# Decay rows of a chunked scan: 128-fold repetition by DMA from a DRAM scratch in place of selector matmuls on TensorE

## The chip, the cores and the metric

The kernel runs on one core of one Trainium2 chip. The metric is the device time of one execution in microseconds. It is given as the median of several runs; a profile is of one further execution. TensorE is called PE (its weight loads PEld), VectorE DVE, ScalarE ACT, GpSimd POOL, SyncE SP.

## The reference

A sequence of 512 tokens of width 1024 goes through two blocks of two layers each. The first block's layer projects the tokens, runs three mixers beside each other (retention, a Mamba-2 scan, attention with forget gates), and projects back. The second block (feed-forward layers and another mixer) is not touched. What matters here is the scan: 16 heads in 2 groups, head width 64, state width 128, chunks of 128 tokens, so 4 chunks.

```python
def step(S, inp):
    xc, ac, bc, cc = inp
    acum = jnp.cumsum(ac, axis=-1)
    seg = acum[..., :, None] - acum[..., None, :]
    Lm = jnp.exp(jnp.where(causal, seg, -jnp.inf))
    cb = jnp.einsum('bign,bjgn->bgij', cc, bc)
    y = jnp.einsum('bgij,bghij,bjghp->bighp', cb, Lm, xc)
    ...
```

For every chunk and head, `seg` is a 128 by 128 matrix of differences of cumulative sums. With one token index on the partitions, the kernel needs `acum` of the other index as a row that stands in all 128 partitions.

## The kernel before

`scan_and_attend` runs once for each of the two layers. Each engine has its own program, and semaphores tie them. PE's matmuls of the input projection (`proj.run`, jobs numbered j, 24 matmuls of 128x256 each for the jobs meant here) are laid between the steps of the scan. Each job writes one of two PSUM banks, and ACT must copy a bank out (`evacuate`) before the second job after it.

The weights come as a stream of units, four jobs to a unit, in two slots. When a unit's last job is done, ACT rounds the next-but-one unit (`round`, line 127, a cast of 128x2048), then POOL subtracts the rounded from the raw weights (`lower`, line 136), and then SP issues the load of the unit after (line 116).

The scan has 8 steps s, one for each chunk c and group g, in the order (0,0), (0,1), (1,0) and so on. In the loop, PE's order in each step is: job A (jv+2+2s), the matmuls of `spread_decay(s + 1)`, job B (jv+3+2s), `outputs(s)`.

- `spread_decay(s)` (line 1169): 8 matmuls, one for each head of the group (the profile shows 16 instructions). The stationary operand is a 16x128 slice of `sel`, a constant with ones in one row; the moving operand is `afm`, the 16 rows of cumulative sums in that chunk. The result, in PSUM banks 4 and 5, is one row of `afm` in all 128 partitions. It waits until ACT has read the banks for the step before.
- `decays(s)` on ACT: 8 activations Relu (line 1347) that read those banks and subtract from the token's own sum, then one Exp over 128x1024 (line 1352), in place in `seg`, which has two buffers. ACT's order in each step is: evacuate A, `decays(s + 1)`, evacuate B, and in every second step (s even) the cast of line 127. From step 3 on ACT loads its function table anew for Exp and for Silu (line 1285).
- `weigh(s)` on DVE (line 1475): multiplies `seg` by the masked products `cb`.
- `outputs(s)` on PE: 8 products of `seg` with x (line 1184), from chunk 1 on the product with the state (1189), and up to chunk 2 the state's new part (1199).
- `combine(s)` on DVE: x times the skip factor (1490), the state's part scaled (1493, reads PSUM) and added (1494), the products added (1495, reads PSUM), the state scaled (1504) and added (1505, reads PSUM). Where a chunk begins, `scale_x` (1467) and `state_input` (1482) follow, and then `weigh(s + 1)`.

`sel` (16x2048, 128 KB) is loaded by SP at the start of the block. `afm` is copied out of PSUM by ACT long before the loop (line 1320). Behind the loop stand the rest of the projection, the norm over the scan's output and the attention.

Of the kernel before, what the change touches and what calls it, by code (L numbers as in the profile page):

```python
# [21 lines left out]
F32 = mybir.dt.float32  # L22
F32R = mybir.dt.float32r
I32 = mybir.dt.int32
ACT = mybir.ActivationFunctionType
AX = mybir.AxisListType

P = 128
T = 512
NT = T // P  # L30
D = 1024
# [11 lines left out]
SH, SP, SG, SN = 16, 64, 2, 128  # L43
HG = SH // SG
# [31 lines left out]
def split3(ap, a):  # L76
    return ap.rearrange("p (a b) -> p a b", a=a)
# [63 lines left out]
def build(nc, dr, out):  # L141
    ctx = ExitStack()
    with ctx:
# [48 lines left out]
        PS = ctx.enter_context(nc.psum_tensor("PS", [P, 8, 512], F32))  # L192
# [23 lines left out]
            return par[:, P2[name][0]:P2[name][1]]  # L216

        phase = [ExitStack()]

        class Arena:  # L220

# [759 lines left out]
        def scan_and_attend(block, l, streams, norm, after):  # L981
# [10 lines left out]
            s_nc, s_ns, s_nu = sem("c_row_loaded"), sem("c_row_activated"), sem("next_ada_used")  # L992
            parts = MixedParts()
            nb = lambda n: sem("ssd_" + n)
            s_sel, s_sv, s_ab, s_ex, s_w1, s_ln = (nb(x) for x in (
                "selectors_loaded", "vector_step", "gate_magnitudes", "gate_exp", "gate_one_plus", "gate_log"))
            s_a, s_lf, s_sm, s_smt, s_ea = (nb(x) for x in (
                "steps_ready", "log_forget_ready", "cumulative_sums", "cumulative_sums_taken", "decays_ready"))
            s_al, s_cv, s_si, s_bt, s_btc = (nb(x) for x in (
                "a_exp", "convolved", "conv_activated", "b_turned", "b_turned_copied"))  # L1000
            s_cb, s_cbm, s_xt, s_xtc, s_xd = (nb(x) for x in (
                "cb_products", "cb_masked", "x_turned", "x_turned_copied", "x_scaled"))
            s_bc, s_sg, s_le, s_we, s_y, s_yt = (nb(x) for x in (
                "log_decay_spread", "log_decay_ready", "decay_ready", "weights_ready", "y_products", "y_taken"))
            s_sd, s_ss2, s_xdd, s_q2, s_r2, s_yn = (nb(x) for x in (
                "state_products", "state_ready", "x_state_scaled", "y_squared", "y_rms", "y_normed"))
            s_tr, s_ev, s_nf = (nb(x) for x in ("y_turned", "y_turned_copied", "negated_copied"))
# [10 lines left out]
            late = A_[:, 0:3 * D + 2 * T + SH * P]  # L1018
# [3 lines left out]
            xdt = split3(late[:, 0:2 * D], 2)  # L1022
            St = split3(late[:, 2 * D:2 * D + 2 * T], 2)
            yt = split3(late[:, 3 * D:3 * D + 2 * T], 2)
            sel = late[:, 4 * D:4 * D + SH * P]
            bcf = split3(m_all[:, 8 * T:12 * T], 4)
            xdd = bcf[:, 0:2, :].rearrange("p a t -> p (a t)")
            fox_v_ = ar.take(4 * T)
# [9 lines left out]
            afm = M[0:SH, 7, :]  # L1038
# [7 lines left out]
            jd, jb, jx, jv, jg, jz, jq, jk, je = (J[x] for x in ("dtf", "bc", "xs", "fv", "fg", "z", "fq", "fk", "out"))  # L1046
            steps = [(c, g) for c in range(NT) for g in range(SG)]
# [13 lines left out]

            @block.sync
            def _(sp):
                sp.dma_start(sel[0:SH, :], dr["sel"]).then_inc(s_sel, 16)
                n = len(stream.units)
                stream.send(sp, RAW, streams.end_in + 2 * SLOTS)
                sp.wait_ge(s_ev, 8)
                if nxt:
                    sp.dma_start(par[:, 0:P1N], of_layer("par1", l + 1)).then_inc(s_par, 16)
                    sp.wait_ge(s_fe, NT)  # L1070
                    sp.dma_start(c_row, dr["c_row"]).then_inc(s_nc, 16)
                    sp.wait_ge(parts.low, 16)
                    for u in range(NEARLY):
                        if u >= 3:
                            sp.wait_ge(s_nu, 2 * (u - 2))
                        sp.dma_start(next_ada[:, u % 3, :], ada_rows(l + 1, u)).then_inc(s_nl[u % 3], 16)
                        stream.send(sp, RAW, streams.end_in + 2 * SLOTS + u + 1)
                else:
                    sp.dma_start(par[:, 0:KD], dr["final_g"]).then_inc(s_par, 16)
                    sp.dma_start(spec[:, 0:C2N], dr["c2"]).then_inc(s_par, 16)  # L1080
                    stream.send(sp, RAW, n)
                for b in range(2):
                    sp.wait_ge(stream.low, n - 1 + b)
                    after.load_first(sp, b)
                sp.wait_ge(s_par, 16 if nxt else 32)
# [21 lines left out]
            def _(pe):  # L1107
# [3 lines left out]
                for c in range(NT):  # L1111
                    last = pe.transpose(PS[:, 7, c * 24:(c + 1) * 24], dtfT[:, c * P:(c + 1) * P],
                                        ident[0:24, 0:24])
# [8 lines left out]
                for c in range(NT):  # L1122
                    last = pe.matmul(PS[0:SH, 5, c * P:(c + 1) * P], aa[:, c, :], triu, start=True, stop=True)
# [32 lines left out]
                    if j - jx >= 2:  # L1156
                        turn_x(j - jx - 2)

                def spread_decay(s):
                    c, g = steps[s]  # L1160
                    if s == 0:
                        pe.wait_ge(s_sel, 16)
                        pe.wait_ge(s_xtc, 8)
                        pe.wait_ge(s_smt, 3)
                    else:
                        pe.wait_ge(s_sg, s)
                    for h in range(HG):
                        hh = g * HG + h
                        last = pe.matmul(PS[:, 4 + h // 4, (h % 4) * P:(h % 4 + 1) * P],
                                         sel[0:SH, hh * P:(hh + 1) * P], afm[:, c * P:(c + 1) * P],  # L1170
                                         start=True, stop=True)
                    last.then_inc(s_bc, 1)

                def outputs(s):
                    c, g = steps[s]
                    pe.wait_ge(s_we, s + 1)
# [22 lines left out]
                        pe.matmul(PS[:, 2 + g, :], bt[:, g, c, :], xdd[:, g * T:(g + 1) * T],  # L1199
                                  start=True, stop=True).then_inc(s_sd, 1)  # L1200

                spread_decay(0)
                for s in range(8):
                    proj.run(pe, jv + 2 + 2 * s, tokens)
                    if s + 1 < 8:
                        spread_decay(s + 1)
                    proj.run(pe, jv + 3 + 2 * s, tokens)
                    outputs(s)
                for j in range(jz + 2, jq + 2):
# [56 lines left out]
            def _(act):  # L1266
# [61 lines left out]
                for g in range(SG):  # L1328
                    act.wait_ge(s_bt, g + 1)
                    act.copy(bt[:, g, :, :], split3(PS[:, 4 + g, 0:384], 3)).then_inc(s_btc, 1)  # L1330
                for j in range(jx, jv + 2):
                    evacuate(j)
                    if 1 <= j - jx < 9:
                        activate(4 + j - jx - 1)
                    if j - jx >= 3:
                        copy_x(j - jx - 3)
                copy_x(7)

                def decays(s):


                    c, g = steps[s]
                    act.wait_ge(s_bc, s + 1)
                    if s >= 2:
                        act.wait_ge(s_y, s - 1)
                    for h in range(HG):
                        last = act.activation(seg[:, s % 2, h * P:(h + 1) * P],
                                              PS[:, 4 + h // 4, (h % 4) * P:(h % 4 + 1) * P], ACT.Relu,
                                              bias=acum[:, c, g * HG + h:g * HG + h + 1], scale=-1.0)
                    last.then_inc(s_sg, 1)  # L1350
                    act.wait_ge(s_sg, s + 1)
                    act.activation(seg[:, s % 2, :], seg[:, s % 2, :], ACT.Exp, scale=-1.0).then_inc(s_le, 1)

                act.wait_ge(s_rn2, 1)
# [1550 lines left out]
def constants():  # L2905

    f = np.float32
    i = np.arange(P)
    c0 = np.zeros((P, C0N), f)
    c0[:, 0:128] = np.eye(P)  # L2910
    c0[:, 128:256] = 1.0
    c0[:, 256:384] = i[:, None] <= i[None, :]
    c0[:, 768:896] = np.where(i[None, :] > i[:, None], -BIG, 0.0)
    c0[:, 896] = (10000.0 ** (-(i % 64) / 64.0)).astype(f)
    c0[:, 897] = np.where(i < 64, -1.0, 1.0)
    c0[:, 899] = 1.0 / (2 * P)
    c0[:, 900] = 1.0 / D
    c1 = np.zeros((P, C1N), f)
    lg = np.log(1.0 - 2.0 ** (-5.0 - np.arange(RH)))
    diff = i[None, :] - i[:, None]  # L2920
    for h in range(RH):
        c1[:, h * P:(h + 1) * P] = np.where(diff >= 0, np.exp(lg[h] * np.maximum(diff, 0)), 0.0) * P ** -0.5
        c1[:, 512 + h * P:512 + (h + 1) * P] = np.exp(lg[h] * (i + 1.0))[None, :]
        c1[:, 1024 + h] = np.exp(lg[h] * (P - 1.0 - i)) * P ** -0.5
    c2 = np.zeros((P, C2N), f)
    t = np.arange(T)
    c2[:, 0:512] = (t % GC != 0)
    for n, w in enumerate((2, 4, 8, 16)):
        a, r = divmod(n, 2)
        c2[64 * r:64 * r + 64, 512 + a * T:512 + (a + 1) * T] = 1.0 / np.minimum(w, t + 1)  # L2930
    for q in range(NT):
        ok = (np.arange(32)[None, :] * CS + CB - 1 <= (q * P + i)[:, None]) & (np.arange(32) < NCMP)[None, :]
        c2[:, 1536 + 32 * q:1568 + 32 * q] = np.where(ok, 0.0, -BIG)
        c2[:, 1664 + 32 * q:1696 + 32 * q] = ok
    c2[:, 1792:2048] = np.tile((np.arange(GC)[None, :] >= i[:, None] % GC), (1, 4))
    sel = np.zeros((SH, SH * P), f)
    for h in range(SH):
        sel[h, h * P:(h + 1) * P] = 1.0
    aug_q, aug_k = np.zeros((40, FH, T), f), np.zeros((40, FH, T), f)
    for h in range(FH):  # L2940
        aug_q[h, h] = -(FD ** 0.5)
        aug_k[32 + h, h] = 1.0
    heads = ((i[:, None] // GV == i[None, :] // GV) / GV).astype(f)
    return dict(c0=c0, c1=c1, c2=c2, heads=heads, sel=sel, aug_q=aug_q.reshape(40, -1), aug_k=aug_k.reshape(40, -1))


def layout(a):
# [84 lines left out]
```

## Time and profile before

| | us |
|---|---|
| median of 3 runs | 3324.16 (3322.51 to 3324.85) |
| the profiled execution | 3324.31 |
| its span, first to last instruction | 3322.1 |
| scan loop, layer 0 | 275.16 to 365.74 |
| scan loop, layer 1 | 846.28 to 937.89 |

Times in the rows are microseconds from the span's start. The profile gives a start and a length for each instruction or group of equal instructions; in brackets stands how long the engine was idle before it, and which engine and line ended that. Issuing a DMA is not counted as busy time.

### The profile page before, as it was taken

Reading aid. Unit: us, or ns where it says so; the run is one execution under the profiler, and the core shown is the slowest. Engines: PE = TensorE matmul, PEld = TensorE weight load, DVE = VectorE, ACT = ScalarE, POOL = GpSimd, SP = SyncE. Lnnn points to the kernel's source line nnn. Section 1 sums busy time; section 2 is a strip of 40 time slices with the busy share of each in tenths; the row PEclk is TensorE's granted clock in tenths of the full one; section 3 lists DMA queues with packets and bytes.
Section 4 is the critical chain, followed back from the end, with each engine's and each line's share of the span. In section 5 each row is a group of like instructions: output and inputs, shape, how many; then the busy total and the mean of one; then the engine's idle time right before and its main releaser. Section 6 shows DMA issues by size and latency. Waiting matters only on the chain. (4 is left out here: it accounts for less than half of the span.)

```text
span 3322.1 us, 40802 instructions
## 1 busy us (share of the span) xinstructions
PE 3131.7 (94%) x16356; PEld 2567.5 (77%) x16356; DVE 1360.1 (41%) x2017; ACT 927.2 (28%) x1647; POOL 1247.4 (38%) x400
## 2 busy tenths in 40 slices
PE   5998989999998999999989999999999998999998
PEld 4878967787887778887766788888888775688886
DVE  6566534737643222223356522233223336642223
ACT  3344443324544211100526311002110244521101
POOL 1322234333223444444440444445444433054442
PEclk9999998999899999999999999999999998999999
DMA  5311222422121122222210122232222211022222
GB/s 225 121 65 51 76 69 95 165 97 76 39 91 66 52 88 88 101 87 88 90 51 14 64 101 89 90 100 89 101 88 88 100 67 48 14 77 101 97 83 73
DMA packets 43467, 279.70 MB, mean 84 GB/s; under 512 B 5241, under 2 KB 5625, under 8 KB 16249
## 3 DMA queue, kind: packets, MB, share of 16 engines
q1 hardware_dynamic: 42688, 270.84, 23.1%
q10 hardware_dynamic: 632, 6.82, 0.7%
q8 instruction: 103, 1.69, 0.2%
q14 instruction: 44, 0.35, 0.0%
HBM read 275.54 MB, written 2.10 MB: 84 GB/s over the span
## 5 line engine op out<-in xcount | busy, mean ns | idle before, releaser
L1877 PE MATMUL PS<-x_parts,w_parts 128*128 128x512 f32 x4224 | 961.0, 390 | 4.0 <-ACT x_parts L726 4.0
L1818 POOL TENSOR_TENSOR w_parts<-w_raw,w_parts 128x2048 fp32r<-128x2048 f32 (+1 forms) x152 | 644.5, 4240 | 810.8 <-DVE w_parts L1952 756.6
L1877 PEld LDWEIGHTS PS<-x_parts,w_parts 128*128 128x128 f32 x4224 | 793.3, 188 | 173.3 <-issue 4.7
L136 POOL TENSOR_TENSOR w_parts<-w_raw,w_parts 128x2048 fp32r<-128x2048 f32 (+1 forms) x98 | 448.1, 4573 | 1053.8 <-ACT w_parts L127 1019.8
L328 PE MATMUL PS<-x_parts,w_parts 128*128 128x512 f32 x2784 | 699.8, 398 | 19.5 <-POOL w_parts L136 10.4
L328 PEld LDWEIGHTS PS<-x_parts,w_parts 128*128 128x128 f32 x2784 | 524.6, 191 | 139.8 <-issue 18.8
L1918 PE MATMUL PS<-hidden_parts,w_parts 128*128 128x512 f32 x2112 | 482.9, 390 | 0.0
L1918 PEld LDWEIGHTS PS<-hidden_parts,w_parts 128*128 128x128 f32 x2112 | 396.2, 188 | 83.9 <-issue 1.9
L1959 DVE TENSOR_TENSOR ffn_buffers<-PS,ffn_buffers 128x512 f32<-128x512 f32 x88 | 60.8, 691 | 732.1 <-PE PS L1877 709.0
L331 PE MATMUL PS<-w_parts,x_parts 128*128 128x256 f32 x2304 | 300.0, 290 | 2.2 <-POOL w_parts L136 2.2
L331 PEld LDWEIGHTS PS<-w_parts,x_parts 128*128 128x128 f32 x2304 | 285.9, 195 | 15.6 <-issue 10.3
L1952 DVE CAST w_parts<-w_raw 128x2048 fp32r<-128x2048 f32 (+1 forms) x144 | 156.8, 1089 | 110.7 <-PE PS L1918 110.7
L127 ACT CAST w_parts<-w_raw 128x2048 fp32r<-128x2048 f32 (+1 forms) x92 | 171.7, 1868 | 88.4 <-PE PS L328 45.7
L1936 ACT CAST hidden_parts<-ffn_buffers 128x512 f32 (+1 forms) x88 | 55.0, 625 | 483.8 <-DVE ffn_buffers L1959 483.8
L1934 ACT ACTIVATE ffn_buffers<-PS 128x512 f32<-128x512 f32 x88 | 52.7, 599 | 338.4 <-PE PS L1877 338.4
L1978 DVE SCALAR_TENSOR_TENSOR x_all<-PS,x_all 128x512 f32<-128x512 f32 x32 | 22.1, 691 | 225.6 <-PE PS L1918 225.6
L1663 ACT ACTIVATE ffn_buffers<-x_all 128x512 f32<-128x512 f32 x28 | 17.6, 632 | 290.5 <-DVE x_all L1978 231.7
L523 ACT ACTIVATE mixer_buffers<-mixer_buffers 128x512 f32<-128x512 f32 (+3 forms) x128 | 70.8, 555 | 38.6 <-DVE mixer_buffers L543 38.6
L328 PE MATMUL PS<-mixed_low,w_parts 128*128 128x512 f32 x192 | 76.4, 398 | 0.0
L299 PE MATMUL PS<-x_parts,w_parts 128*128 128x512 f32 x192 | 56.4, 423 | 16.7 <-ACT x_parts L1768 8.6
L543 DVE CUSTOM_DVE_ANT_0 mixer_buffers<-PS,cst 128x512 f32<-128x512 f32 (+3 forms) x128 | 57.6, 487 | 30.9 <-PE PS L470 30.9
L480 PE MATMUL PS<-cst,mixer_buffers 128*128 128x128 f32 x320 | 52.6, 294 | 16.3 <-ACT mixer_buffers L523 12.8
(394 smaller groups left out, 3197.2 us busy)
## 6 DMA issues: line engine op xcount, KB each, us to landing
w_raw<-in_w_gu SPq DMA_DIRECT2D x88, 1024.0 KB, 4.8
w_raw<-in_w_in SPq DMA_DIRECT2D x70, 1024.0 KB, 4.8
w_raw<-in_w_d SPq DMA_DIRECT2D x64, 704.0 KB, 4.0
w_raw<-in_w_out SPq DMA_DIRECT2D x24, 1024.0 KB, 4.8
m_all<-in_w_next SPq DMA_DIRECT2D x14, 1024.0 KB, 8.2
m_all<-in_w_gate SPq DMA_DIRECT2D x8, 1024.0 KB, 4.9
m_all<-in_w_next ACTq DMA_DIRECT2D x2, 1024.0 KB, 11.2
x_all<-in_x ACTq DMA_DIRECT2D x1, 2048.0 KB, 13.2
```

Of the source, the lines that this page charges most:

```text
L127: op(parts[:, self.slot(u), 0, 0:n], raw[:, self.slot(u), 0:n]).then_inc(self.high, 1)
L136: pool.tensor_tensor(parts[:, self.slot(u), 1, 0:n], raw[:, self.slot(u), 0:n], parts[:, self.slot(u), 0, 0:n].bitcast(F32), ALU.subtract) ...
L299: pe.matmul(PS[0:m, self.bank(j), :], w[:, k, c:c + m], XS[:, 0, k, :], start=(n == 0 and a == 0), stop=False)
L328: last = pe.matmul(PS[0:m, self.bank(j), :], w[a][:, k, c:c + m], part(b, k), start=start, stop=stop)
L331: last = pe.matmul(PS[:, j % 2, 0:m], part(a, k)[:, c * P:(c + 1) * P], w[b][:, k, :], start=start, stop=stop)
L523: act.activation(self.p[:, s % 2, b, 0:n], self.p[:, s % 2, b, 0:n], ACT.Exp, bias=self.nm[:, at:at + 1], scale=-1.0, accum_out=self.rs(s, ...
L543: dve.tensor_tensor_reduce(self.p[:, s % 2, b, 0:n], PS[:, 2 * (s % 2) + b, 0:n], const("causal")[:, T - n:T], -(HD ** -0.5), 3.0e38, ALU. ...
L1818: pool.tensor_tensor(WP[:, b, 1, 0:n], RAW[:, b, 0:n], WP[:, b, 0, 0:n].bitcast(F32), ALU.subtract).then_inc(self.low, 1)
L1877: return pe.matmul(PS[:, 2 * b + g, :], WP[:, slot(b), w, c:c + P], XS[:, x, k, :], start=start, stop=stop)
L1918: last = pe.matmul(PS[:, 4 + m % 2, :], WP[:, slot(b), w, k * P:(k + 1) * P], hid[:, x, b * KH + k, :], start=(b == k == n == 0), stop=(b ...
L1952: dve.tensor_copy(WP[:, slot(b), 0, 0:n], RAW[:, slot(b), 0:n]).then_inc(self.high, 1)
L1959: dve.tensor_tensor(pt[:, b, :], PS[:, 2 * b + 1, :], gs[:, b, :], ALU.mult).then_inc(self.product, 1)
```

## The change

The cumulative sums are stored once for each layer to a scratch tensor in DRAM, by a DMA that ACT issues after its copies of line 1330. From there ACT loads, for each step, one row of 1024 numbers repeated over 128 partitions (512 KB) into one of two buffers `rows`, which take the room of `sel`. The loads of steps 0 and 1 are issued before job jx+2 is copied out, behind a wait for the store. The load of step s+2 is issued in `decays(s)` between the Relu group and the Exp. The Relu activations read `rows` in place of PSUM. The matmuls of `spread_decay`, their waits and `sel` with its load are gone.

```diff
+        decay_rows = nc.dram_tensor("decay_rows", (NT, SH * P), F32, kind="Internal").ap()
...
-            sel = late[:, 4 * D:4 * D + SH * P]
+            rows = split3(late[:, 4 * D:6 * D], 2)
...
-                sp.dma_start(sel[0:SH, :], dr["sel"]).then_inc(s_sel, 16)
...
-                def spread_decay(s):
-                    c, g = steps[s]
-                    if s == 0:
-                        pe.wait_ge(s_sel, 16)
-                        pe.wait_ge(s_xtc, 8)
-                        pe.wait_ge(s_smt, 3)
-                    else:
-                        pe.wait_ge(s_sg, s)
-                    for h in range(HG):
-                        hh = g * HG + h
-                        last = pe.matmul(PS[:, 4 + h // 4, (h % 4) * P:(h % 4 + 1) * P],
-                                         sel[0:SH, hh * P:(hh + 1) * P], afm[:, c * P:(c + 1) * P],
-                                         start=True, stop=True)
-                    last.then_inc(s_bc, 1)
...
-                spread_decay(0)
                 for s in range(8):
                     proj.run(pe, jv + 2 + 2 * s, tokens)
-                    if s + 1 < 8:
-                        spread_decay(s + 1)
                     proj.run(pe, jv + 3 + 2 * s, tokens)
                     outputs(s)
...
+                act.dma_start(decay_rows.rearrange("c (h j) -> h c j", h=SH),
+                              split3(afm, NT)).then_inc(s_dw, 16)
+                def load_decays(s):
+                    c, g = steps[s]
+                    source = decay_rows[c:c + 1, g * D:(g + 1) * D].broadcast_to([P, D])
+                    act.dma_start(rows[:, s % 2, :], source).then_inc(s_dr[s % 2], 16)
+
                 for j in range(jx, jv + 2):
+                    if j == jx + 2:
+                        act.wait_ge(s_dw, 16)
+                        for s in range(2):
+                            load_decays(s)
                     evacuate(j)
...
-                    act.wait_ge(s_bc, s + 1)
+                    act.wait_ge(s_dr[s % 2], 16 * (s // 2 + 1))
                     if s >= 2:
                         act.wait_ge(s_y, s - 1)
                     for h in range(HG):
                         last = act.activation(seg[:, s % 2, h * P:(h + 1) * P],
-                                              PS[:, 4 + h // 4, (h % 4) * P:(h % 4 + 1) * P], ACT.Relu,
+                                              rows[:, s % 2, h * P:(h + 1) * P], ACT.Relu,
                                               bias=acum[:, c, g * HG + h:g * HG + h + 1], scale=-1.0)
                     last.then_inc(s_sg, 1)
                     act.wait_ge(s_sg, s + 1)
+                    if s + 2 < 8:
+                        load_decays(s + 2)
                     act.activation(seg[:, s % 2, :], seg[:, s % 2, :], ACT.Exp, scale=-1.0).then_inc(s_le, 1)
```

## Rows read from the trace of the kernel before

**Rows 1.** The page: busy time of each engine and share of the span.

```profile
PE 3131.7 (94%) x16356; PEld 2567.5 (77%) x16356; DVE 1360.1 (41%) x2017; ACT 927.2 (28%) x1647; POOL 1247.4 (38%) x400
```

**Rows 2.** Windows of the two scan loops: busy us (instructions) by engine; clock; DMA.

```profile
275.16:365.74 90.58, 90.58 (x665) 83.08 (x665) 55.11 (x50) 51.52 (x102) 19.50 (x4) 0.96 0.10 36
846.28:937.89 91.61, 91.61 (x665) 84.03 (x665) 55.12 (x50) 51.57 (x102) 19.52 (x4) 0.95 0.10 36
```

**Rows 3.** Timeline of PE, steps 2 and 3, layer 0: start, length, line.

```profile
304.50 2.05 PE L1169 MATMUL PS<-m_all,ssd_buffers 16*128 16x128 f32 x16
306.47 3.13 PE L331 MATMUL PS<-w_parts,x_parts 128*128 128x256 f32 x24
309.44 1.89 PE L1184 MATMUL PS<-ssd_buffers,m_all 128*128 128x64 f32 x16
...
312.54 3.42 PE L331 MATMUL PS<-w_parts,x_parts 128*128 128x256 f32 x24
315.89 2.05 PE L1169 MATMUL PS<-m_all,ssd_buffers 16*128 16x128 f32 x16
```

**Rows 4.** Timeline of PE, start of the loop, layers 0 and 1.

```profile
275.16 3.75 PE L1169 MATMUL PS<-m_all,ssd_buffers 16*128 16x128 f32 x16 [0.72 <-issue]
...
288.35 1.89 PE L1184 MATMUL PS<-ssd_buffers,m_all 128*128 128x64 f32 x16
...
860.49 1.89 PE L1184 MATMUL PS<-ssd_buffers,m_all 128*128 128x64 f32 x16
```

**Rows 5.** Windows after the restart; behind the five busy times the granted clock.

```profile
278.80:282.00 3.20, 3.20 (x16) 3.16 (x16) 0.00 (x0) 2.98 (x9) 0.00 (x0) 0.50 0.01 3
282.00:284.00 2.00, 2.00 (x16) 1.87 (x16) 0.35 (x1) 1.87 (x3) 0.00 (x0) 0.93 0.00 0
855.30:857.50 2.20, 2.20 (x17) 2.01 (x16) 1.57 (x2) 0.37 (x1) 0.00 (x0) 0.90 0.00 0
```

**Rows 6.** Timeline of ACT and POOL, steps 2 to 4, layer 0.

```profile
304.60 0.37 ACT L1282 COPY ssd_buffers<-PS 128x256 f32<-128x256 f32 x1 [5.05 <-PE PS L331]
306.58 2.17 ACT L1347 ACTIVATE m_all<-PS,m_all 128x128 f32<-128x128 f32 x8 [1.60 <-PE PS L1169]
308.78 1.06 ACT L1352 ACTIVATE m_all<-m_all 128x1024 f32<-128x1024 f32 x1
...
310.00 1.90 ACT L127 CAST w_parts<-w_raw 128x2048 fp32r<-128x2048 f32 x1
...
320.17 1.28 ACT L1352 ACT_TABLE_LOAD   x1
...
311.97 4.58 POOL L136 TENSOR_TENSOR w_parts<-w_raw,w_parts 128x2048 fp32r<-128x2048 f32 x1 [16.52 <-ACT w_parts L127]
```

**Rows 7.** Timeline of DVE, steps 2 to 4, layer 0.

```profile
312.36 0.69 DVE L1493 TENSOR_TENSOR ssd_buffers<-PS,m_all 128x512 f32<-128x512 f32 x1 [5.73 <-PE PS L1189]
313.08 4.03 DVE L1494 TENSOR_TENSOR ssd_buffers<-ssd_buffers 128x512 f32<-128x512 f32 x1
...
319.31 1.22 DVE L1475 TENSOR_TENSOR m_all<-m_all,ssd_buffers 128x1024 f32<-128x1024 f32 x1
...
323.75 0.69 DVE L1493 TENSOR_TENSOR ssd_buffers<-PS,m_all 128x512 f32<-128x512 f32 x1 [2.62 <-PE PS L1189]
...
329.65 1.22 DVE L1475 TENSOR_TENSOR m_all<-m_all,ssd_buffers 128x1024 f32<-128x1024 f32 x1
```

**Rows 8.** DMA issues of the page, and a DMA issue and a wait behind the loop.

```profile
ssd_buffers<-in_c_row SPq DMA_DIRECT2D x1, 512.0 KB, 3.3
...
407.57 0.56 ACTq L1365 DMA_DIRECT2D ssd_buffers<-in_aug_q  x1
...
419.86 3.40 DVE L1527 TENSOR_SCALAR ssd_buffers<-m_all 8x4096 f32<-8x4096 f32 x1 [12.37 <-DMA ssd_buffers<-in_aug_k]
```

**Rows 9.** Timeline of PE around a short gap, layer 1.

```profile
830.55 0.63 PE L1150 MATMUL PS<-cst,ssd_buffers 128*128 128x128 f32 x4 [1.94 <-ACT ssd_buffers L1306]
830.94 4.61 PE L331 MATMUL PS<-w_parts,x_parts 128*128 128x256 f32 x24
```

More of the change, by code:

```diff
@@ L994, in scan_and_attend @@
             nb = lambda n: sem("ssd_" + n)
-            s_sel, s_sv, s_ab, s_ex, s_w1, s_ln = (nb(x) for x in (
-                "selectors_loaded", "vector_step", "gate_magnitudes", "gate_exp", "gate_one_plus", "gate_log"))
+            s_dw, s_dr = nb("decays_stored"), [nb(f"decays_loaded_{i}") for i in range(2)]
+            s_sv, s_ab, s_ex, s_w1, s_ln = (nb(x) for x in (
+                "vector_step", "gate_magnitudes", "gate_exp", "gate_one_plus", "gate_log"))
             s_a, s_lf, s_sm, s_smt, s_ea = (nb(x) for x in (
@@ L1002, in scan_and_attend @@
                 "cb_products", "cb_masked", "x_turned", "x_turned_copied", "x_scaled"))
-            s_bc, s_sg, s_le, s_we, s_y, s_yt = (nb(x) for x in (
-                "log_decay_spread", "log_decay_ready", "decay_ready", "weights_ready", "y_products", "y_taken"))
+            s_sg, s_le, s_we, s_y, s_yt = (nb(x) for x in (
+                "log_decay_ready", "decay_ready", "weights_ready", "y_products", "y_taken"))
             s_sd, s_ss2, s_xdd, s_q2, s_r2, s_yn = (nb(x) for x in (
@@ L2935, in constants @@
     c2[:, 1792:2048] = np.tile((np.arange(GC)[None, :] >= i[:, None] % GC), (1, 4))
-    sel = np.zeros((SH, SH * P), f)
-    for h in range(SH):
-        sel[h, h * P:(h + 1) * P] = 1.0
     aug_q, aug_k = np.zeros((40, FH, T), f), np.zeros((40, FH, T), f)
@@ L2943, in constants @@
     heads = ((i[:, None] // GV == i[None, :] // GV) / GV).astype(f)
-    return dict(c0=c0, c1=c1, c2=c2, heads=heads, sel=sel, aug_q=aug_q.reshape(40, -1), aug_k=aug_k.reshape(40, -1))
+    return dict(c0=c0, c1=c1, c2=c2, heads=heads, aug_q=aug_q.reshape(40, -1), aug_k=aug_k.reshape(40, -1))
 def layout(a):
```

## The prediction

> **What bounds the kernel now.** I read the page first: PE is busy for 94% of the span, all others for less than half [rows 1]. That is an average, so I took the windows of the two scan loops next. PE is busy there without a gap, 90.58 of 90.58 us and 91.61 of 91.61 us, while DVE has 55 us of work, ACT 52 and POOL 20 [rows 2]. So in the loop a microsecond of PE work less is a microsecond less, until another engine's chain is late. The timelines say how near those chains are. From row to row one spreading costs PE 1.97 us (304.50 to 306.47), job B 2.97, the outputs 3.10 (309.44 to 312.54) and job A, which begins behind outputs, 3.35 [rows 3]. A step is 11.39 us.
>
> **What is removed.** Eight spreadings in each layer. Seven are worth 1.97 us each. The first runs at 1.2 GHz: it takes 3.75 us [rows 4], since PE was idle before, and the granted clock is 0.50 until the first window of rows 5 ends and a little into the second. The second (0.93 over 2.00 us, so 0.28 us more at half clock) puts the return to 2.4 GHz at 282.28 in layer 0; the third (0.90 over 2.20 us) puts it at 855.74 in layer 1 [rows 5]. I take that these times don't move when other matmuls fill the stretch. Then the first spreading too is worth its full-clock work, 1.97 us, since what follows moves into the slow stretch in its place. PE also loses a wait: the first spreading stood until ACT's last copy of x, 0.72 us [rows 4]; job A needs no such copy. At half clock that is 0.36 us of work. So each layer loses 8 x 1.97 + 0.36 = 16.1 us. For layer 0 this puts the first outputs 4.3 us before their 288.35, for layer 1 as much before 860.49 [rows 4]. The load of `sel` goes too. I count it at nothing: it stands ahead of loads that SP sends only when POOL has freed a slot. If it were, 128 KB are a quarter of the 512 KB that land in 3.3 us [rows 8], under 1 us a layer.
>
> **What is added on ACT.** The Relu group waited 1.60 us in every step for the spreading [rows 6]. It now follows the copy of A at once. Against that stands the issue of a DMA between Relu and Exp. Issuing on ACT took 0.56 us for a 640 KB load [rows 8]; I take 0.4 us, between nothing and that. The first two loads and the store are issued long before the loop and cost ACT at most 3 x 0.56 us, in a stretch where ACT is idle before its copies; I count nothing, and up to 1.7 us a layer as the bound. The Relus read SBUF in place of PSUM. The row has 2.17 us for eight [rows 6]; I keep it. The Trainium skill speaks against this (VectorE: DVE Perf Modes, The TRN2 errata): a ScalarE instruction has a fixed part of 224 cycles from SBUF and 172 from PSUM, at 1.2 GHz. By that eight would cost 0.35 us more, no row here shows it, and an estimate of the sum by it is under 1 us higher.
>
> **The loads.** None in the trace reads one row 128 times. The nearest row by size, 512 KB in 128 rows, lands after 3.3 us; the slowest is the pair of 640 KB behind the loop, for which DVE waits 12.37 us [rows 8]. The store is smaller than any of them. A load is issued in `decays(s)` and wanted in `decays(s + 2)`, two steps later, some 20 us. Both bounds are hidden, so I count nothing. The store (32 KB) has the time from line 1330 to job jx+2, two projection jobs.
>
> **What is late next.** Call b the end of job B in an even step s of chunks 1 to 3. PE by itself would want `seg` of step s+1 at b + 3.10 + 3.35 + 2.97 = b + 9.42 [rows 3].
>
> DVE's chain begins with line 1493, at 312.36, so 2.92 behind b = 309.44 [rows 7, 3]. In even steps it meets POOL. Line 1494 takes 4.03 us in place of 0.69: it ends 0.56 us after POOL's line 136, which ran from 311.97 for 4.58 us [rows 7, 6]. The two don't run side by side. Before, `weigh(3)` ended at 319.31 + 1.22 = 320.53 [rows 7], and PE wanted it at 315.89 + 1.97 + 2.97 = 320.83 [rows 3]. The slack was 0.3 us. Now PE wants it 1.97 us sooner.
>
> POOL's start moves too. From the end of A, ACT's chain is 0.10 + 0.27 (copy) + 2.20 (Relus) + 0.40 (issue) + 1.22 (Exp and copy of B) + 1.97 (cast, to POOL's start) = 6.16 us [rows 6], and A ends at b - 2.97: POOL runs from b + 3.19 to b + 7.77. Line 1494, due at b + 3.64, waits for it. Then 0.56 for its end, three operations at 0.72 (313.08 less 312.36), and 1.22: `weigh(3)` ends at b + 7.77 + 0.56 + 2.16 + 1.22 = b + 11.7, that is **2.3 us late**.
>
> In step 4 two table loads of 1.28 us [rows 6] stand in ACT's chain, so POOL starts at b - 2.97 + 6.16 + 2.56 = b + 5.75. The five short operations of `combine` are through at b + 2.92 + 5 x 0.72 = b + 6.5. Now `weigh(5)` waits for POOL (to b + 10.33) and ends near b + 11.55: **2.1 us late**.
>
> From step 3 to 4 there is no POOL, but `scale_x` and `state_input` stand before `weigh`: from 323.75 to 329.65 + 1.22 it is 7.12 us [rows 7]. PE comes back 0.18 + 3.35 + 2.97 = 6.50 us after that same start (312.36 against 312.54 in step 2) [rows 3, 7]: **0.6 us late**. For steps 0 to 1 the same sum comes out just in time, since PE's half clock gives ACT and POOL room; from 5 to 6 `state_input` is gone, and in step 6 `combine` is three operations, so `weigh(7)` is through before POOL starts. So 5.0 us a layer are waits in place of work.
>
> **Sum.** 2 x (16.1 - 5.0) = 22.2 us less. The long waits are new gaps of 2.1 to 2.3 us for PE, four in all. After a gap of 1.94 us the rows show one job at 4.61 us in place of 3.13, with the clock down for a part of it [rows 9, 3]; I allow for one such fall, 1.5 us. Behind the loop all chains hang on the last jobs, so the gain passes on. The profiled execution took 3324.3 us (span 3322.1 and 2.2 around it), which stands 0.15 us over the median. 3324.3 - 22.2 + 1.5 = 3303.6, for the median, rounded, **3304 us**, 0.6% less. A measurement here can tell some 0.2%, 6.6 us, from no change.
>
> **Rivals.**
>
> - *The gain comes whole.* DVE and POOL don't meet as I have it, because ACT's cast comes later (a longer issue) or DVE takes its turn first. Then all 32.2 us come: 3292 us. For it: DVE has only 55 us of work in a loop of 75 [rows 2]. Against it: `weigh(3)` had 0.3 us of slack, and the lock is in every even step's rows. 12%.
> - *The clock takes part of it back.* Each of the four gaps brings PE to 1.2 GHz. One fall costs 1.5 us [rows 9], or, at the loop's start, the slow stretch of 7.1 us from 275.16 to 282.28 costs half of it, 3.6 us [rows 4, 5]. Four falls are 6 to 14 us: 3308 to 3317. 17%. The Trainium skill (TensorE: Matmul & The Clock Gate, What's actually happening) has it that the slow state is the default and activity lifts it; by that, new gaps in a loop that had none are the danger. The trace agrees so far as its falls stand behind idle time.
> - *The loads come late*, and it is slower than before. If reading one row 128 times made a load last L, each pair of steps would last about L + 3.4 us (Relus, Exp) with the issue of the next. Before, a pair took 22.8 us. From L near 20 us the wait decides. At 25 us a pair takes 28.4 us, 5.6 more than before; three pairs in each of two layers give 34 us, and the loop's start gives back 4.3 us each time: 3324 + 34 - 9 = 3349 us. For it: no row shows such a read, and the pair of 12.37 us shows that layout can cost a lot. Against it: 16 queues are busy for a tenth in the loop [rows 2]. 4%.
> - *It moves nothing.* Another wait behind the loop, set by a transfer whose time doesn't move, takes the gain. I found none. 6%.
>
> **Chances and range.** My forecast has 61%. Its own range is 3298 to 3309, from the unknown issue (0 to 0.56 us moves POOL's start and with it each of four waits), the Relus and a fall more or less. For 8 in 10 the range reaches down to the whole gain and up to the clock's upper end: 3290 to 3317. Faster by over 0.2% (below 3317.5) are the forecast, the whole gain and nearly all of the clock's rival: 88%. Within 0.2%: 8%. Slower: 4%.
>
> **What would show it.** Line 1169 is gone; the loop of layer 0, job A to the last outputs, takes about 80 us. PE shows gaps of 2.1 to 2.3 us before line 1184 in steps 3 and 5 and of 0.6 us in step 4, ended by DVE's line of `weigh`, and in those steps a DVE operation on two SBUF operands ends just behind POOL's. No wait of ACT for a DMA in the loop. The granted clock shows whether a gap cost more than its length. The prediction is wrong if PE waits for ACT (loads late, Relus longer), if the gaps last much more or less than this, or if the stretch from the last outputs to the attention grows.

## The result, and the profile after

The changed kernel takes 3306.91 us (median of 5 runs, 3304.90 to 3307.43), the kernel before 3324.16 us beside it. The ratio is 0.9946, with a 95% interval of 0.9933 to 0.9959: 17 us or 0.5% less. The forecast was 3304 us. Its profiled execution took 3304.9 us, with a span of 3302.7 us, 19.4 us less than before.

The windows of the two loops, from job A of step 0 to the end of the last outputs, answer to [rows 2]:

```profile
274.70:358.04 83.34, 77.82 (x538) 70.11 (x537) 58.13 (x50) 53.31 (x103) 19.04 (x4) 0.91 0.23 76
836.05:917.58 81.53, 76.11 (x538) 68.33 (x537) 57.45 (x50) 53.32 (x103) 18.60 (x4) 0.94 0.24 78
```

PE is no longer busy for the whole loop: 77.82 of 83.34 us, and 76.11 of 81.53. From the restart of PE ahead of each loop (the transposes of x, 273.35 and 844.47 before, 273.96 and 835.31 after) to the start of the last outputs it was 90.15 and 91.18 us, and is 81.84 and 80.03 us. That is 8.31 and 11.15 us less, together 19.46 us, and so the whole difference of the spans. What lies ahead of the loops, between and behind them kept its length within 1.5 us.

The timeline of PE in both loops, against [rows 3, 4]:

```profile
282.83 1.89 PE L1170 MATMUL PS<-ssd_buffers,m_all 128*128 128x64 f32 x16
...
302.71 6.30 PE L332 MATMUL PS<-w_parts,x_parts 128*128 128x256 f32 x48
311.89 2.00 PE L1170 MATMUL PS<-ssd_buffers,m_all 128*128 128x64 f32 x16 [2.87 <-DVE m_all L1471]
...
322.91 1.89 PE L1170 MATMUL PS<-ssd_buffers,m_all 128*128 128x64 f32 x16
...
334.96 3.67 PE L1170 MATMUL PS<-ssd_buffers,m_all 128*128 128x64 f32 x16 [2.65 <-DVE m_all L1471]
...
843.49 2.00 PE L1170 MATMUL PS<-ssd_buffers,m_all 128*128 128x64 f32 x16
...
872.67 2.64 PE L1170 MATMUL PS<-ssd_buffers,m_all 128*128 128x64 f32 x16 [2.89 <-DVE m_all L1471]
...
884.41 2.00 PE L1170 MATMUL PS<-ssd_buffers,m_all 128*128 128x64 f32 x16 [0.54 <-DVE m_all L1471]
...
895.90 2.03 PE L1170 MATMUL PS<-ssd_buffers,m_all 128*128 128x64 f32 x16 [1.98 <-DVE m_all L1471]
```

Jobs A and B now run as one (48 matmuls, 6.15 us from start to start). The first outputs come at 282.83, 8.87 us after the restart, where it was 15.00; in layer 1 it is 8.18 us against 16.02. PE waits for `weigh` (now line 1471) ahead of step 3 in both layers (2.87, 2.89 us), ahead of step 5 (2.65, 1.98 us), and in layer 1 ahead of step 4 (0.54 us). That makes 10.93 us of gaps.

DVE and POOL around steps 2 to 4 of layer 0, against [rows 7, 6]:

```profile
302.53 0.69 DVE L1489 TENSOR_TENSOR ssd_buffers<-PS,m_all 128x512 f32<-128x512 f32 x1 [3.57 <-PE PS L1175]
303.25 5.15 DVE L1490 TENSOR_TENSOR ssd_buffers<-ssd_buffers 128x512 f32<-128x512 f32 x1
...
310.61 1.22 DVE L1471 TENSOR_TENSOR m_all<-m_all,ssd_buffers 128x1024 f32<-128x1024 f32 x1
...
329.44 5.47 DVE L1471 TENSOR_TENSOR m_all<-m_all,ssd_buffers 128x1024 f32<-128x1024 f32 x1
...
303.25 4.61 POOL L136 TENSOR_TENSOR w_parts<-w_raw,w_parts 128x2048 fp32r<-128x2048 f32 x1 [11.09 <-ACT w_parts L127]
329.25 4.57 POOL L136 TENSOR_TENSOR w_parts<-w_raw,w_parts 128x2048 fp32r<-128x2048 f32 x1 [21.40 <-ACT w_parts L127]
```

Line 1490 (1494 before) starts together with POOL's subtraction and takes 5.15 us in place of 0.69. It ends 0.54 us behind POOL. `weigh(3)` stands behind it in the queue and ends at 311.83; PE's outputs start at 311.89. In step 4 POOL starts later and `weigh(5)` itself is held up: it takes 5.47 us in place of 1.22 and ends 1.09 us behind POOL.

ACT in step 2, against [rows 6]; then the loads and the store as the page lists them (KB each, median us to landing):

```profile
297.20 2.45 ACT L1341 ACTIVATE m_all<-ssd_buffers,m_all 128x128 f32<-128x128 f32 x8
299.68 0.33 ACTq L1319 DMA_DIRECT2D ssd_buffers<-decay_rows  x1
300.05 1.06 ACT L1348 ACTIVATE m_all<-m_all 128x1024 f32<-128x1024 f32 x1 [0.40 <-ACT m_all L1341]
```

```profile
ssd_buffers<-decay_rows ACTq DMA_DIRECT2D x16, 512.0 KB, 4.1
...
decay_rows<-m_all ACTq DMA_DIRECT2D x2, 32.0 KB, 1.6
```

The eight Relus take 2.45 us, where they took 2.17. Between them and the Exp the DMA's issue takes 0.33 us, and ACT is idle for 0.40. A load lands 4.1 us after its issue (3.3 to 5.8 over all sixteen). ACT wants it 10.2 us after the issue at the earliest (in layer 1, issued at 839.40 and read from 849.57), and no wait of ACT for one is in the trace.

Last the windows of the granted clock (the number behind the five busy times), at the loop's start and around the gap ahead of step 3 in layer 0, and one at the loop's start in layer 1:

```profile
274.00:278.00 4.00, 4.00 (x19) 4.00 (x20) 2.30 (x2) 3.49 (x11) 0.00 (x0) 0.50 0.01 2
278.00:280.00 2.00, 2.00 (x12) 2.00 (x11) 0.06 (x1) 1.60 (x3) 0.00 (x0) 0.52 0.44 174
280.00:282.00 2.00, 2.00 (x19) 2.00 (x19) 1.15 (x2) 2.00 (x6) 0.00 (x0) 1.00 0.23 88
...
311.80:314.00 2.20, 2.11 (x17) 2.08 (x18) 0.64 (x2) 1.52 (x2) 0.00 (x0) 1.00 0.68 266
314.00:316.20 2.20, 2.20 (x5) 0.82 (x3) 0.68 (x1) 0.00 (x0) 0.00 (x0) 0.51 0.01 2
316.20:318.50 2.30, 2.30 (x14) 1.78 (x13) 2.16 (x5) 0.00 (x0) 0.00 (x0) 0.72 0.00 0
318.50:322.00 3.50, 3.50 (x32) 3.50 (x31) 3.46 (x4) 1.77 (x7) 0.00 (x0) 1.00 0.02 5
...
838.00:840.00 2.00, 2.00 (x12) 2.00 (x12) 1.42 (x2) 1.61 (x6) 0.00 (x0) 0.57 0.00 0
```

The granted clock is 0.50 (1.2 GHz) to 278.0, and 0.52 in the window that follows: with 1.92 of its 2 us at half clock that is 1 - 0.96/2, so full clock is back at 279.9, 6.0 us after the restart. Before it was back at 282.28 [rows 5], 8.9 us after. In layer 1 it is 4.4 us (0.57 in the last row) in place of 11.3, worked out in the same way. These starts repeat well: over the eight profiled executions whose start of the loop is that of the changed kernel (this one, its repeat and six of the experiments below), the first outputs come 8.0 to 8.9 us after the restart. But a new half-clock stretch stands behind the gap: 0.51 from 314.0 to 316.2, and 0.72 in the next window, 1.3 us of its 2.3. From 311.89 to 322.91, start of outputs to start of outputs, the step takes 11.02 us, where 9.25 us are its work (what the same step takes in the weigh-first run below, without a gap and at full clock).

### The profile page after: what moved, and what is told of

Same layout as the page of the kernel before. It is cut to its first block and busy times, and to the rows that moved or that the text cites. A ratio compares the mean times of both kernels' runs of the same rounds, so it can differ in the third digit from the quotient of the medians.

```text
span 3302.7 us, 40306 instructions
## 1 busy us (share of the span) xinstructions
PE 3103.2 (94%) x16100; PEld 2538.9 (77%) x16100; DVE 1371.0 (42%) x2017; ACT 929.6 (28%) x1647; POOL 1246.2 (38%) x400
## 3 DMA queue, kind: packets, MB, share of 16 engines
HBM read 283.67 MB, written 2.16 MB: 87 GB/s over the span
```

## The experiments

There are eleven runs. One of them repeats the changed kernel, and one repeats an earlier experiment beside it. Ratios are to the kernel before on the same chip. "Loop" means from PE's restart to the start of the last outputs, for layers 0 and 1. The loop times of the kernel before are 90.15 and 91.18 us, of the changed one 81.84 and 80.03.

**The matmuls back, unread.** The stationary operand is a piece of the identity, the moving one `afm` as before.

```diff
+                idle_products(0)
                 for s in range(8):
                     proj.run(pe, jv + 2 + 2 * s, tokens)
+                    if s + 1 < 8:
+                        idle_products(s + 1)
                     proj.run(pe, jv + 3 + 2 * s, tokens)
                     outputs(s)
```

> The changed kernel with matmuls of the old size (16 rows, 8 for each step) back in their old places; nobody reads them, ACT still takes the rows from the DMA. My theory (the gain is PE work taken away, less new gaps): the loops are full again, the gaps before line 1184's successor go, 3321 to 3327 us. Rival (the gain is ACT's earlier start, or the first steps' missing wait, and the matmuls themselves were free): it stays near 3307.

Measured: 3325.54 us, ratio to before 1.0006 (0.9996 to 1.0015); loops 91.63 and 92.55 us. PE's timeline, steps 1, 2 and 7:

```profile
304.27 2.05 PE L1194 MATMUL PS<-m_all,cst 16*128 16x128 f32 x16
306.25 3.13 PE L332 MATMUL PS<-w_parts,x_parts 128*128 128x256 f32 x24
...
364.83 2.00 PE L1170 MATMUL PS<-ssd_buffers,m_all 128*128 128x64 f32 x16 [1.39 <-DVE m_all L1483]
...
359.98 4.79 DVE L1483 TENSOR_TENSOR m_all<-m_all,ssd_buffers 128x1024 f32<-128x1024 f32 x1
...
358.71 4.98 POOL L136 TENSOR_TENSOR w_parts<-w_raw,w_parts 128x2048 fp32r<-128x2048 f32 x1 [17.93 <-ACT w_parts L127]
```

The whole gain is gone, with the DMA, its issue and ACT's early start in place. So the gain is PE's matmuls (and the wait of the first of them, which is back too), and in the time of the whole kernel the DMA side costs nothing that can be measured. The loops are 1.5 and 1.4 us longer than in the kernel before, and that is one gap in each, ahead of step 7: POOL's subtraction starts at 358.71 and `weigh(7)`, which comes behind it, takes 4.79 us in place of 1.23. In the kernel before POOL starts at 360.35, 0.17 us behind `weigh(7)` (360.18). ACT no longer waits for the spreading, so its cast and with it POOL come sooner: the early start is no gain here, it moves POOL's work onto what PE needs.

**Weigh first.** DVE does `scale_x` and `weigh` of step s+1 ahead of `combine` of step s, in the idle time in which it waits for the outputs.

```diff
-                    weigh(s)
-                    combine(s)
+                    if s + 1 < 8:
+                        if g == 0:
+                            scale_x(c)
+                        weigh(s + 1)
+                    combine(s)
+                    if s + 1 < 8 and g == 0 and c < NT - 1:
+                        state_input(c)
```

Here c and g are those of step s+1; step 0 is prepared ahead of the loop.

> DVE's order in the changed kernel: scale_x and weigh of step s+1 stand before combine of step s, where DVE is idle. My theory (the gaps of PE come from weigh queued behind operations that POOL's subtraction holds up, and the clock falls behind those gaps): both gaps in each layer shrink to 0.4 us or less, 10 us of gaps and most of 8 us of slow clock come back, 3288 to 3293 us. Rival (weigh isn't the cause, the wait moves to the y that must be taken out of PSUM or to the state): gaps of over 1.5 us stay, 3303 to 3309.

Measured: 3283.97 us, ratio 0.9878 (0.9863 to 0.9894); loops 71.27 and 70.95 us. PE, DVE and POOL in step 3 of layer 0, and the windows of both loops from step 1 on:

```profile
308.31 1.97 PE L1170 MATMUL PS<-ssd_buffers,m_all 128*128 128x64 f32 x16 [0.23 <-issue]
...
300.27 1.23 DVE L1471 TENSOR_TENSOR m_all<-m_all,ssd_buffers 128x1024 f32<-128x1024 f32 x1 [3.85 <-ACT m_all L1348]
...
302.86 4.63 DVE L1490 TENSOR_TENSOR ssd_buffers<-ssd_buffers 128x512 f32<-128x512 f32 x1
...
302.30 4.63 POOL L136 TENSOR_TENSOR w_parts<-w_raw,w_parts 128x2048 fp32r<-128x2048 f32 x1 [11.43 <-ACT w_parts L127]
...
283.00:346.25 63.25, 63.02 (x478) 57.59 (x477) 51.84 (x47) 45.44 (x83) 17.97 (x4) 1.00 0.27 92
834.00:896.00 62.00, 61.76 (x467) 56.33 (x465) 51.19 (x47) 45.21 (x83) 17.34 (x4) 1.00 0.28 94
```

`weigh(3)` is done at 301.50, before POOL starts. DVE is still held up (4.63 us at line 1490), but only `combine` is queued behind it. PE waits 0.23 us, until `combine` has read its PSUM bank (to 308.21). No half clock follows: the granted clock is 1.00 over both windows. The loops are 10.6 and 9.1 us shorter than in the changed kernel, 19.7 us in sum: the 10.9 us of gaps and the 8.7 us of clock behind them, worked out below. The time is 4 us under the expected range. That range counted from the median of 3307 us; from the profiled execution of the changed kernel, 3304.9 us, the same 19.7 us lead to 3285.2, and the profiled execution here took 3285.03.

**The same order in the kernel before.**

> The same order of DVE in the kernel before. My theory (there PE never waited for DVE): no change, 3321 to 3327 us. Rival (the order is worth the same in both, so that the change of the matmuls isn't what made it late): 3305 to 3315.

Measured: 3323.82 us, ratio 1.0000 (0.9990 to 1.0009); loops 90.10 and 90.96 us. The order is worth nothing while PE is full. It is worth some 20 us once the matmuls are gone.

**POOL writes only.** For the four weight units of each loop POOL writes zeros and reads nothing; the low part of these weights is missing from the result.

```diff
+            if u in getattr(self, "plain", ()):
+                pool.memset(parts[:, self.slot(u), 1, 0:n].bitcast(F32), 0.0).then_inc(self.low, 1)
...
+            stream.plain = {proj.jobs[j][0] for j in (jg, jg + 4, jz, jz + 4)}
```

> The changed kernel, in which POOL, for the four weight units that it treats inside each loop, writes zeros in place of the difference, so that it reads nothing from SBUF; the low part of those weights is left out of the result. My theory (DVE stands still because POOL's subtraction reads SBUF through what DVE's second operand needs): DVE's operations of 5.1 and 5.5 us take 0.7 and 1.2 us, the gaps of steps 3 and 5 go, one of 0.5 us in step 4 may stay, 3286 to 3292 us. Rival (DVE's chain is too long by itself, or writing is enough to hold it up): gaps of 1.5 us and more stay, 3300 to 3309.

Measured: 3286.48 us, ratio 0.9879 (0.9856 to 0.9902); loops 71.68 and 71.45 us. PE, DVE and POOL, layer 0:

```profile
318.30 2.00 PE L1175 MATMUL PS<-ssd_buffers,m_all 128*128 128x64 f32 x16 [0.68 <-DVE m_all L1476]
...
302.61 0.69 DVE L1495 TENSOR_TENSOR ssd_buffers<-ssd_buffers 128x512 f32<-128x512 f32 x1
...
305.50 1.23 DVE L1476 TENSOR_TENSOR m_all<-m_all,ssd_buffers 128x1024 f32<-128x1024 f32 x1
...
302.58 1.81 POOL L137 MEMSET w_parts<- 128x2048 f32 x1 [14.17 <-ACT w_parts L127]
```

Line 1495 (1490 in the changed kernel) takes 0.69 us although POOL is at work from 302.58 to 304.39, and `weigh` takes 1.23. The order of DVE is the changed kernel's. So what made `weigh` late in steps 3 and 5 was POOL's reading, and not the length of DVE's chain; and the 0.6 us of step 4, without POOL, came out as forecast (0.68). `weigh(5)` takes 1.23 us here too, with POOL at work beside it (324.94, POOL from 323.78 to 325.59). POOL's work is also shorter here, 1.81 us in place of 4.6. That alone would have made the hold-up shorter, but not zero. The Trainium skill (SBUF — State Buffer, Who interferes with whom) has the rule: a DVE instruction with two SBUF inputs contends with a GpSimd instruction that reads SBUF, and not with one that only writes it. The trace agrees: 5.15 us beside the reader, 0.69 us beside the writer.

**The gaps filled.** Two unread matmuls of 128x512 ahead of the wait in steps 3 and 5 (x4 in the rows: each has two records).

```diff
                 def outputs(s):
                     c, g = steps[s]
+                    if s in (3, 5):
+                        keep_busy(pe, 4, 2)
                     pe.wait_ge(s_we, s + 1)
```

> The changed kernel with two unread 128x512 matmuls (2.05 us at 2.4 GHz) ahead of the wait for seg in steps 3 and 5, in a PSUM bank that the change left free. My theory (8 us of the loops are half clock that follows the gaps): the gaps' length stays, filled for the most part, the clock stays at 2.4 GHz, 3298 to 3302 us. Rival 1 (the clock falls for another reason): no gain, 3305 to 3311. Rival 2 (the clock falls anyway since the rest of the gap is enough): 3303 to 3307.

Measured: 3300.16 us (3295.16 to 3313.05), ratio 0.9926 (0.9914 to 0.9939); loops 78.57 and 76.80 us, 6.5 us less than in the changed kernel. Step 3 of layer 0, then of layer 1:

```profile
307.90 1.88 PE L579 MATMUL PS<-cst 128*128 128x512 f32 x4
310.93 2.04 PE L1172 MATMUL PS<-ssd_buffers,m_all 128*128 128x64 f32 x16 [1.15 <-DVE m_all L1473]
...
315.50 6.65 PE L332 MATMUL PS<-w_parts,x_parts 128*128 128x256 f32 x48
...
868.68 1.88 PE L579 MATMUL PS<-cst 128*128 128x512 f32 x4
871.71 2.00 PE L1172 MATMUL PS<-ssd_buffers,m_all 128*128 128x64 f32 x16 [1.15 <-DVE m_all L1473]
...
874.92 6.32 PE L332 MATMUL PS<-w_parts,x_parts 128*128 128x256 f32 x48
```

In layer 1 the clock stays up: outputs 3.21 us to the start of jobs A and B (871.71 to 874.92), and 6.32 us for these. In layer 0, with the same rest of 1.15 us of idle time, it fell all the same (4.57 us from outputs to jobs, 310.93 to 315.50, in place of 3.21, and 6.65 us for the jobs). It didn't fall behind step 5 in either layer. So filling the gaps took away three falls of four, and it is no sure cure. How strong that is, the gaps left open tell: in six profiled executions in which nothing fills them (the changed kernel twice, 16 and 128 rows ahead of the loop, the issue behind the Exp twice) there are 24 gaps of 1.96 to 2.89 us ahead of steps 3 and 5, and the clock fell behind 22. It stayed up behind two, of 2.16 and 1.96 us, ahead of step 5 in the second run of the issue behind the Exp. So most of the half clock does come from the gaps, but a gap of this length makes a fall likely and not certain. The runs of this kernel spread over 18 us, and its profiled execution, the slowest, lost 12 us behind the loops, where it does not differ from the changed one; I rest on the loops.

**One set of matmuls ahead of the loop alone,** once with 16 rows and once with 128 (the identity times a constant). Both have back the wait for the last copy of x.

```diff
+                idle_products(0)
                 for s in range(8):
```

> The changed kernel with one set of 16-row matmuls, as the first spreading was, and its wait for the last copy of x, back ahead of the loop alone. My prediction's theory (the clock comes back at the same time whatever PE runs): 2 x (1.97 + 0.36) = 4.7 us more, 3311 to 3313, and the half clock ends as early after the restart as in the changed kernel, 4 to 5 us. Rival (these matmuls are why the half clock lasted 9 and 11 us): 5 us a layer more, 3315 to 3319, with the half clock at 9 to 11 us again.

> The same place and number of matmuls, but over all 128 rows. Both theories: 3311 to 3314, half clock for 4 to 6 us after the restart. If 16 rows cost the same as this, the rows don't matter; if 16 rows cost 4 to 6 us more than this, they do.

Measured: 3316.82 us, ratio 0.9976 (0.9965 to 0.9988), for 16 rows; 3314.82 us, ratio 0.9975 (0.9967 to 0.9984), for 128. The two medians can't be told apart, and both runs spread over 17 us; the 16 rows lie in the range of their rival, the 128 rows a little over the one range given for them. The piece from the restart to the first outputs is clearer. It is 8.87 and 8.18 us in the changed kernel, 13.01 and 13.68 us with 16 rows, 10.75 and 12.03 us with 128: 9.6 us more in sum, and 5.7 us. The windows of the granted clock of layer 0, with 16 rows:

```profile
278.00:280.00 2.00, 2.00 (x10) 1.78 (x10) 0.00 (x0) 1.90 (x2) 0.00 (x0) 0.50 0.55 219
280.00:282.00 2.00, 2.00 (x11) 2.00 (x11) 1.46 (x2) 0.44 (x1) 0.00 (x0) 0.50 0.11 43
282.00:284.00 2.00, 2.00 (x15) 2.00 (x14) 0.36 (x1) 0.03 (x1) 0.00 (x0) 0.76 0.00 0
```

and with 128 rows:

```profile
273.00:275.00 2.00, 1.32 (x6) 0.93 (x6) 0.46 (x1) 1.49 (x4) 0.00 (x0) 0.50 0.00 0
275.00:278.00 3.00, 3.00 (x18) 3.00 (x18) 1.90 (x2) 2.61 (x8) 0.00 (x0) 0.60 0.07 12
278.00:280.00 2.00, 2.00 (x19) 2.00 (x18) 0.31 (x1) 1.58 (x2) 0.00 (x0) 1.00 0.73 248
```

With 16 rows the half clock ends at 283.0, 9.3 us after the restart (273.64), with 128 rows at 277.4, 4.6 us after its restart (272.80). In layer 1 the windows put it 10.9 and 7.5 us behind the restart. In layer 1, where the gap ahead of the restart is the same (5.64 and 5.61 us), half clock thus lasted 3.4 us longer with 16 rows. In layer 0 the 128-row kernel's own gap was shorter (5.60 us against 7.08), so the 4.7 us there are not a clean comparison. The direction speaks for the rows; but it is one profiled execution each, and the 128-row kernel's two layers differ by 2.9 us, so neither the size nor the cause is settled.

**The issue behind the Exp,** twice, the second time beside the changed kernel.

```diff
-                    if s + 2 < 8:
-                        load_decays(s + 2)
                     act.activation(seg[:, s % 2, :], seg[:, s % 2, :], ACT.Exp, scale=-1.0).then_inc(s_le, 1)
+                    if s + 2 < 8:
+                        load_decays(s + 2)
```

> The load of step s+2 is issued behind the Exp in place of ahead of it. My theory: the 0.40 us between Relu and Exp go from ACT's path to the cast only in part, since the issue still stands ahead of the cast; Exp ends 0.4 us sooner, POOL starts at the same time, so the gaps stay and the time stays within 2 us of 3307. Rival (PE waits for the Exp through DVE): four gaps shorter by 0.4 us and smaller clock falls, 3303 to 3305.

> The changed kernel itself, beside the next one. Both theories: 3304 to 3308 us. Its spread is what the comparison with the next one needs.

> The issue behind the Exp once more, on the same chip as the changed kernel. My theory (its loops were 1.8 us shorter, so the rest of the 5.8 us was the spread between chips and runs): 1 to 3 us under the changed kernel. Rival (the issue ahead of Exp costs what that run showed): 5 to 7 us under it.

Measured: 3301.13 us, ratio 0.9929 (0.9916 to 0.9943), and the second time 3300.26 us, ratio 0.9931 (0.9905 to 0.9957); the changed kernel beside it 3303.82 us, ratio 0.9936 (0.9916 to 0.9956). I had expected the gaps to stay. They are a little shorter: 2.52 us in place of 2.87 and 2.89 ahead of step 3, since ACT no longer stands idle for 0.40 us between Relu and Exp and POOL starts that much sooner. The medians are 5.8 and 3.6 us lower, but the intervals overlap, and the second time the loops differ mostly by the clock: they are 77.56 and 77.45 us, against 79.99 and 79.94 in the repeat of the changed kernel, 4.9 us less, and 3.3 us of that are step 5, where the clock did not fall this time. Its windows, from outputs to outputs:

```profile
332.70:342.10 9.40, 9.38 (x69) 8.42 (x70) 6.75 (x9) 4.48 (x12) 0.00 (x0) 1.00 0.30 108
903.10:912.46 9.36, 9.36 (x69) 8.40 (x69) 6.71 (x9) 4.63 (x12) 0.00 (x0) 1.00 0.27 105
```

The first of the two runs also has a new gap of 0.73 us ahead of step 1 in layer 0. So what the place of the issue is worth is not settled.

**Both edits together.**

> The DVE order of the weigh-first run together with the DMA issue behind the Exp. The weigh-first run had two gaps of 0.23 us and a half clock only at the loop's start. My theory (what is left there is PE work): 3282 to 3285 us, no better than weigh first alone. Rival (the issue ahead of the Exp costs by itself, as the 3301 us of that run seemed to say): 3277 to 3280.

Measured: 3282.08 us, ratio 0.9873 (0.9851 to 0.9896); loops 70.58 and 70.45 us, with no gap left. It can't be told from weigh first alone. Either is 1.2% under the kernel before and 0.6 to 0.7% under the changed one.

## Why the prediction was right, and which of its terms were off

**PE bounds the loop, and its matmuls are the gain.** Right, by the first experiment. One spreading was put at 1.97 us. It is worth 2.14: in the weigh-first run a step takes 9.25 us from outputs to outputs (of [rows 3] it was 11.39), because A and B now run on without a seam.

**The loop's start.** The step "these times don't move when other matmuls fill the stretch" failed. Put at 4.3 us a layer, it gave 6.1 and 7.8 us: the clock came back at 279.9, not at 282.3, 3.0 us sooner after the restart, and in layer 1 6.9 us sooner. Half clock does half the work, so that is worth 1.5 and 3.5 us beside the 4.3, 5.8 and 7.8 in all; 0.3 us of layer 0 are left. The two layers gave 5.3 us more than forecast. Why the clock came back sooner is not shown; the runs with one set of matmuls ahead of the loop only narrow it down.

**The DMA side costs nothing.** Right: 4.1 us to landing (5.8 at the most) against 10.2 us of cover at the least (the prediction had put it at some 20), and 3325.5 us with the matmuls back. The issue was put at 0.4 us and took 0.40. The Relus were kept at 2.17 us and take 2.45. The estimate from the Trainium skill (VectorE: DVE Perf Modes, The TRN2 errata), 0.35 us more, was the better one; the measured 0.28 stands in its place.

**Weigh comes late behind POOL.** Right in place and cause (POOL writes only, weigh first), and nearly in size: ahead of step 3 2.3 us were forecast and 2.87 and 2.89 came, ahead of step 5 2.1 against 2.65 and 1.98, ahead of step 4 0.6 against 0 and 0.54 (in layer 0 half clock makes PE itself late enough). In sum 10.0 us against 10.9. Of the 0.6 us that step 3 was short, the Relus explain 0.28 and PE's quicker return 0.17.

**The clock falls.** One fall at 1.5 us was allowed for. There were four, one behind each long gap: steps 3 and 5 take 11.02 and 12.45 us in layer 0, 11.20 and 11.05 us in layer 1, less 9.25 us each: 8.7 us. This is the rival that I gave 17%: its mechanism came true, its 3308 to 3317 us did not. The clock took 7.2 us more than the forecast allowed for, the start gave 5.3 us more and the steps 2.0 us more (12 times 0.17). That these cancel to within 0.1 us is luck; the sum came out nearer than its terms.

The sum with measured sizes: 12 x 2.14 + 6.1 + 7.8 less 10.9 of gaps and 8.7 of clock is 20.0 us, against 19.46 measured in the loops. The rest of 0.5 us is covered by the seam that a gap opens: without a gap the outputs start some 0.15 us before the row of the job ahead of them ends (291.22 against 285.07 + 6.31 = 291.38), so each of the five gaps costs some 0.15 us over its bracket, 0.8 us in all.

**The rivals.** The gain did not come whole by itself, but it is there to be had: 3292 us were put at it, and weigh first gave 3284, since the start's larger share comes on top. The loads did not come late. Nothing behind the loop took the gain.

## What to carry to other kernels

Taking work off the engine that bounds a stage is worth that work only until the next engine's chain is late; compare that chain's end with the time at which the bounding engine would come back, step by step, before and after. Where it comes out late, look at the order of the late engine's queue: here one operation that had long been ready stood behind others that another engine could hold up, and moving it gave about as much again as the change itself (19.7 us of the loops, after 19.5). An order that changes nothing in the kernel before can be worth most in the kernel after.

## What the runs showed of the hardware

- Behind gaps of only 2 to 2.9 us of PE, in loops where it was busy otherwise, the granted clock went to half (1.2 GHz) in all four cases of the profiled execution, at 1.8 to 3.2 us each (the step's length less 9.25 us), and in 22 of 24 over six profiled executions. With the gaps filled but for 0.26 to 1.15 us it fell in one case of four.
- The length of half clock behind a restart changed with what ran first: 8.9 and 11.3 us in the kernel before, 9.3 and 10.9 us with one set of 16-row matmuls, but 6.0 and 4.4 us in the changed kernel, and 4.6 and 7.5 us with 128 rows. Why is not shown.
- A DVE operation on two SBUF operands takes 5.15 us beside a POOL subtraction of 4.61 us, and 0.69 us beside a POOL memset of 1.81 us.
- A load of 512 KB that reads one DRAM row 128 times landed after 4.1 us (3.3 to 5.8 over sixteen), against 3.3 us [rows 8] and 5.9 us for the two loads of 512 KB from 128 separate rows in the kernel before.
